# Four chunks of each input projection computed from split rows and split weights, with the VectorE taps dealt anew

## What is computed

```python
def hybrid_layer(h, p_i, prev_a, prev_c, g_mix, w_in, w_conv_a, w_s, b_s, g_ln_b, b_ln_b,
                 w_conv_c, b_conv_c, g_ln_c, b_ln_c, g_out, w_o, g_ffn, ffn,
                 g_ple, w_ple_gate, w_ple_proj):
    n = rmsnorm(h, g_mix)
    z = n @ w_in
...
    conv_a, new_a = causal_dwconv(gate_c * xa, prev_a, w_conv_a)
    y_a = gate_b * conv_a
    zb = jax.nn.gelu(z[..., o3:o4])
...
    y_b = u * chunk_mix(v, w_s, b_s)
    zc = z[..., o4:]
    glu = zc[..., :D_C] * jax.nn.sigmoid(zc[..., D_C:])
    conv_c, new_c = causal_dwconv(glu, prev_c, w_conv_c)
    y_c = jax.nn.silu(layernorm(conv_c + b_conv_c, g_ln_c, b_ln_c))
...
    h = h + y @ w_o
    h = h + ffn(rmsnorm(h, g_ffn))
```

## Time and profile before

| | us |
|---|---|
| three executions | 1082.21, 1084.42, 1085.61 |
| their median | 1084.42 |
| the profiled execution | 1082.2 |
| its span in the trace | 1080.6 |
| input projection, layer 0, in the trace | 9.4 to about 85 |
| input projection, layer 1, in the trace | 338.4 to about 416 |

### The profile page before, as it was taken

One profiled execution on the slowest core, in us unless ns is written; L12 is line 12 of the kernel. 1 busy time (PEld: TensorE's weight loads), 2 busy tenths in 40 slices (PEclk: granted clock), 3 DMA queues, 4 the chain that ended last, 5 costly groups with the idle time before them and its releaser, 6 DMA issues.

```text
span 1080.6 us, 16287 instructions
## 1 busy us (share of the span) xinstructions
PE 1063.3 (98%) x5883; PEld 921.4 (85%) x5883; DVE 886.3 (82%) x1300; ACT 682.0 (63%) x875; POOL 43.8 (4%) x58
## 2 busy tenths in 40 slices
PE   9999999999999999999999999999999999999996
PEld 8888999999999888788888888888888888878786
DVE  5898866566677888569989899898998999999775
ACT  2117544344454116458888888888888878888674
POOL 1000000000000000000010000100100001003000
PEclk9999999999999999999999999999999999999998
DMA  8442645545444433439999999999999999999921
GB/s 336 153 156 82 232 170 217 204 168 212 167 156 156 152 110 116 185 127 391 352 383 398 335 412 364 367 399 363 390 370 359 403 363 379 377 366 405 385 88 41
DMA packets 24197, 291.50 MB, mean 270 GB/s; under 512 B 3160, under 2 KB 3192, under 8 KB 7376
## 3 DMA queue, kind: packets, MB, share of 16 engines
q1 hardware_dynamic: 21040, 280.32, 67.7%
q0 software_dynamic: 3104, 10.46, 2.8%
HBM read 283.98 MB, written 6.79 MB: 269 GB/s over the span
## 4 chain that ended last, share of the span: by engine, by line
PE 92%; DVE 4%; ACT 2%; DMA 1%; issue 1%; POOL 0%; DVEq 0%; ACTq 0%; POOLq 0%
PE bank L672 16%; PE bank L676 16%; PE bank L675 15%; PE bank L721 13%; PE bank L745 8%; PE bank L748 8%; PE bank L749 8%; PE bank L761 2%; PE bank L616 1%; DMA ring<-wstream 1%; DVE cv L1498 1%; PE bank L600 1%; PE bank L581 1%; DVE wlo L1324 0%; PE bank L783 0%
## 5 line engine op out<-in xcount | busy, mean ns | idle before, releaser
L1324 DVE TENSOR_TENSOR wlo<-ring,whi 128x1024 fp32r<-128x1024 f32 x384 | 459.9, 1221 | 49.6 <-ACT whi L919 42.8
L919 ACT ACTIVATE whi<-ring 128x1024 fp32r<-128x1024 f32 x384 | 404.3, 1059 | 85.3 <-PE bank L672 72.3
L672 PE MATMUL bank<-whi,gh_hi 128*128 128x512 f32 x512 | 204.4, 399 | 0.1
L676 PE MATMUL bank<-whi,gh_lo 128*128 128x512 f32 x512 | 199.7, 390 | 0.0
L675 PE MATMUL bank<-wlo,gh_hi 128*128 128x512 f32 x512 | 199.5, 390 | 0.0
L745 PE MATMUL bank<-gh_hi,whi 128*128 128x264 f32 x480 | 138.0, 288 | 0.0
L748 PE MATMUL bank<-gh_lo,whi 128*128 128x264 f32 x480 | 136.0, 283 | 0.0
L749 PE MATMUL bank<-gh_hi,wlo 128*128 128x264 f32 x480 | 135.9, 283 | 0.0
L672 PEld LDWEIGHTS bank<-whi,gh_hi 128*128 128x128 f32 x512 | 96.2, 188 | 21.9 <-DVE wlo L1324 3.5
L676 PEld LDWEIGHTS bank<-whi,gh_lo 128*128 128x128 f32 x512 | 96.1, 188 | 20.9
L675 PEld LDWEIGHTS bank<-wlo,gh_hi 128*128 128x128 f32 x512 | 96.3, 188 | 18.4
(11 more groups left out here) (278 smaller groups left out, 1373.5 us busy)
## 6 DMA issues: line engine op xcount, KB each, us to landing
ring<-wstream SPq DMA_DIRECT2D x130, 2048.0 KB, 8.4
y_rows<-work POOLq DMA_DIRECT2D x7, 512.0 KB, 8.2
ring<-wstream SPq DMA_DIRECT2D x1, 1536.0 KB, 10.2
h<-x_in SPq DMA_DIRECT2D x2, 528.0 KB, 4.1
y_out<-work SPq DMA_DIRECT2D x2, 528.0 KB, 3.0
par<-par_in SPq DMA_DIRECT2D x2, 494.5 KB, 6.9
c_sample<-xc POOLq DMA_DIRECT2D x2, 372.0 KB, 3.6
stc<-state_in SPq DMA_DIRECT2D x2, 360.0 KB, 9.4
```

What stands on the lines that cost most here:

```text
L672: mm = pe.matmul(out[:, :], xh, whi[:, pos, cols_], start=(k == 0), stop=False)
L676: mm = pe.matmul(out[:, :], xl, whi[:, pos, cols_], start=False, stop=(k == last))
L919: nc.scalar.activation(whi[:, q % SPLITS, :], quarter_at(q), ACT.Copy).then_inc(S["hi"], 1)
L1324: v.tensor_tensor(wlo[:, q % SPLITS, :], quarter_at(q), whi[:, q % SPLITS, :].bitcast(F32), ALU.subtract).then_inc(S["lo"], 1)
```

## The change

`SPLIT_FROM = 9`: chunks `zab` 9 to 12 of both layers are computed by `project` from high and low parts of rows and weights. Their quarters drop out of `in_fp32` (`EARLY_SPLIT`), so the splitting of weights covers them. The rows' high parts, `gh_hi`, are copies of `gz` by ScalarE (`high_rows`), their low parts, `gh_lo`, subtractions by VectorE (`low_rows`); in layer 0 all eight stand behind the reciprocal root's guess, in layer 1 four ahead of it and four behind. The states are copied by ScalarE. The taps between the evacuations are 8, 8, 8, 8, then 7 and 5, then 4 each, where they were 7, 7, 7, 7, then 6 and 5 throughout. Some semaphores are merged (`ones_ready` into `consts`, `y_hi` and `y_lo` into `rows_hi` and `rows_lo`), with their counts.

```diff
+SPLIT_FROM = 9
+EARLY_SPLIT = [NEED[_b["zab"] + _c] - 1 for _b in BASE for _c in range(SPLIT_FROM, N_ZAB)]
+
+
 def in_fp32(q):
-    return any(0 <= q - a < n for a, n in zip(FP32_FROM, FP32_Q))
+    return q not in EARLY_SPLIT and any(0 <= q - a < n for a, n in zip(FP32_FROM, FP32_Q))
...
+                def projected(first, end):
+                    for c in range(first, end):
+                        if c < SPLIT_FROM:
+                            project_fp32(B["zab"] + c, 1, gz)
+                        else:
+                            project(B["zab"] + c, 1, *ghs, rows_lo if c == SPLIT_FROM else None, waited=KD * 2 * l)
+
+                projected(0, 2 * CB)
...
+                def high_rows(first, end):
+                    for k in range(first, end):
+                        act.wait_ge(S["gh_mix"], k + 1)
+                        nc.scalar.activation(gh_hi[:, k, :], gz[k], ACT.Copy).then_inc(rows_hi, 1)
+
+                if l:
+                    act.wait_ge(acc_ready, BASE[0]["ple"] + KD)
+                high_rows(0, ROWS_FIRST[l])
                 guess_of(bank[4], root[:, :], rstd[:, :], (S["ms"], 1), S["root"])
+                high_rows(ROWS_FIRST[l], KD)
+                act.wait_ge(loaded[l], 48)
+                if l:
+                    act.wait_ge(L[l - 1]["tails"], 1)
+                nc.scalar.activation(xa[:, :, :, 0:TAPS_A - 1], sta[:, :, :, :], ACT.Copy).then_inc(states_copied, 1)
+                nc.scalar.activation(xc[:, :, :, 0:TAPS_C - 1], stc[:, :, :, :], ACT.Copy).then_inc(states_copied, 1)
...
-                def states():
-
-                    dve.wait_ge(loaded[l], 48)
-                    if l:
-                        dve.wait_ge(L[l - 1]["tails"], 1)
-                    nc.vector.tensor_copy(xa[:, :, :, 0:TAPS_A - 1], sta[:, :, :, :])
-                    link(nc.vector.tensor_copy(xc[:, :, :, 0:TAPS_C - 1], stc[:, :, :, :]))
-
+                def low_rows(first, end):
+                    for k in range(first, end):
+                        dve.wait_ge(rows_hi, KD * 2 * l + k + 1)
+                        nc.vector.tensor_tensor(gh_lo[:, k, :], gz[k], gh_hi[:, k, :].bitcast(F32),
+                                                ALU.subtract).then_inc(rows_lo, 1)
+
+                low_rows(0, ROWS_FIRST[l])
                 reciprocal_root((S["root"], 1), bank[4])
+                low_rows(ROWS_FIRST[l], KD)
...
                 for c in range(2 * CB):
                     evacuate(B["zab"] + c, ycat[:, c, :])
-                    some_taps(4)
-                    low_upto(dense_quarters(B["zab"] + c))
-                    some_taps(3)
+                    some_taps(8)
...
                 for c in range(CA):
                     evacuate(at + 2 * c, pp[:, 6, :])
-                    some_taps(3)
+                    some_taps(4 if c else 7)
                     low_upto(dense_quarters(at + 2 * c))
-                    some_taps(3)
...
-                    some_taps(5)
+                    some_taps(4 if c else 5)
```

More of the change, by code:

```diff
@@ L86 @@
 EARLY_Q = (40, 45)
+ROWS_FIRST = (0, 4)
 GROUP_ORDER = (2, 0, 1)
@@ L298, in build @@
         late_step = sem("overflow_step")
+        rows_hi, rows_lo = sem("high_parts_of_rows"), sem("low_parts_of_rows")
+        states_copied = sem("states_copied")
         guessed = sem("reciprocal_root_guessed")
@@ L307, in build @@
             "y_c", "y_a", "y_b", "ys_sq", "y_ms", "y_root", "y_normed", "sq_ffn",
-            "gh_ple", "sq_ple", "sig_ple", "tails", "w_sT", "y_hi", "y_lo")} for l in range(DEPTH)]
+            "gh_ple", "sq_ple", "sig_ple", "tails", "w_sT")} for l in range(DEPTH)]
         L[0].update({n: sem(n) for n in ("gh_ffn", "silu", "hid_f32", "hid_hi", "hid", "hid2")})
@@ L424, in _ @@
             for d, t in ones.items():
-                pool.memset(t[:, :], 1.0 / d).then_inc(ones_ready, 1)
+                pool.memset(t[:, :], 1.0 / d).then_inc(consts, 1)
             pool.memset(eps[:, :], EPS).then_inc(consts, 1)
@@ L438, in _ @@
                       allow_small_or_imprecise_dtypes=True).then_inc(consts, 1)
-            pool.wait_ge(consts, 10)
+            pool.wait_ge(consts, 14)
             pool.affine_select(out=ident[:, :], in_=ident[:, :], compare_op=ALU.not_equal, fill=1.0,
@@ L724, in project_fp32, with project @@
                     mm.then_inc(acc_ready, 1)
-            def project(first_chunk, n_chunks, hi, lo, waits=None, S=dense, after=None):
+            def project(first_chunk, n_chunks, hi, lo, waits=None, S=dense, after=None, waited=0):
                 for i in range(n_chunks):
@@ L742, in project @@
                         if i == 0 and waits:
-                            pe.wait_ge(waits, k + 1)
+                            pe.wait_ge(waits, waited + k + 1)
                         wh, wl = block_of(S, q, w)
@@ L780, in _ @@
             mix = both(hid_hi, hid_lo, KD)
-            pe.wait_ge(ones_ready, len(ones))
+            pe.wait_ge(consts, len(ones))
             for _ in range(WARM_UP):
                 pe.matmul(bank[7][:, 0:P], ones[1][:, :], ones[1][:, :], start=True, stop=True)
-            pe.wait_ge(consts, 13)
+            pe.wait_ge(consts, 17)
             for l in range(DEPTH):
@@ L792, in _ @@
                 project_fp32(B["zc"] + 1, N_ZC - 1, gz)
[L793 removed]
+                def projected(first, end):
[5 more added lines that the diff above has]
+                projected(0, 2 * CB)
                 average(bank[5], D_B, [zb[:, c, :] for c in range(CB)], S["mean"], (S["gelu"], 1))
[L796 removed]
+                projected(2 * CB, 2 * CB + 2)
                 pe.wait_ge(S["squared"], 1)
                 average(bank[5], D_B, [sq[:, c, :] for c in range(CB)], S["variance"])
[L799 removed]
+                projected(2 * CB + 2, N_ZAB - 2)
                 pe.wait_ge(S["ln_b"], CB)
@@ L806, in _ @@
                 mm.then_inc(S["vt"], 1)
-                project_fp32(B["zab"] + N_ZAB - 2, 1, gz)
+                projected(N_ZAB - 2, N_ZAB - 1)
                 average_c = [cv[:, c, :] for c in range(CC)]
@@ L822, in _ @@
                 average(bank[5], D_C, [sq[:, CA + CB + c, :] for c in range(CC)], S["variance"])
-                project_fp32(B["zab"] + N_ZAB - 1, 1, gz)
+                projected(N_ZAB - 1, N_ZAB)
                 pe.wait_ge(loaded[l], 48)
@@ L845, in _ @@
                     else:
-                        project(B["wo"] + k, 1, *mix, S["y_lo"] if k == WO_FP32 else None)
+                        project(B["wo"] + k, 1, *mix, rows_lo if k == WO_FP32 else None, waited=KD * (2 * l + 1))
                     if l and k:
@@ L1033, in final_rows @@
                 nc.scalar.activation(ycat[:, k, :], h[:, k, :], ACT.Copy, scale=col(0, "g_final", k)).then_inc(y_gained, 1)
-            act.wait_ge(consts, 13)
+            act.wait_ge(consts, 17)
             nc.scalar.activation(warm[:, 0:1], eps[:, :], ACT.Abs_reciprocal_sqrt)
@@ L1107, in _ @@
                     act.wait_ge(S["y_normed"], ROW_ORDER.index(k) + 1)
-                    nc.scalar.activation(hid_hi[:, k, :], ycat[:, k, :], ACT.Copy).then_inc(S["y_hi"], 1)
+                    nc.scalar.activation(hid_hi[:, k, :], ycat[:, k, :], ACT.Copy).then_inc(rows_hi, 1)
                 for k in range(KD):
@@ L1455, in add_to_h @@
                 dve.wait_ge(acc_evac, chunk + 1)
-            dve.wait_ge(consts, 13)
+            dve.wait_ge(consts, 17)
             dve.wait_ge(par_loaded[0], 16)
@@ L1503, in _ @@
                     if c == 0:
-                        states()
+                        dve.wait_ge(states_copied, 2 * l + 2)
                     some_taps(6 if c else 0, c)
@@ L1632, in _ @@
                 for k in range(KD):
-                    dve.wait_ge(S["y_hi"], k + 1)
+                    dve.wait_ge(rows_hi, KD * (2 * l + 1) + k + 1)
                     nc.vector.tensor_tensor(hid_lo[:, k, :], ycat[:, k, :], hid_hi[:, k, :].bitcast(F32),
-                                            ALU.subtract).then_inc(S["y_lo"], 1)
+                                            ALU.subtract).then_inc(rows_lo, 1)
                 dve.wait_ge(acc_evac, B["wo"])
```

4 lines of the change are left out of this document (removed).

## The result

The changed kernel takes 1086.22 us (median, 1084.38 to 1087.62) beside 1083.79 us before (1082.21 to 1086.25, measured with it). The ratio is 1.0022 with an interval of 1.0015 to 1.0029: 1.6 to 3.1 us slower, small but real, and inside the 0.3% that was set as "no change". The forecast was +1.6 us and a median of 1086.0. Of all executions reported here one was in the chip's slower state, one of e0's twelve, with 1179.28 us at a mean granted clock of 0.85; e0's ratio leaves it out.

A forecast was written before the change was run, and what follows sets the result against it. The end of VectorE's taps, not TensorE, was taken to bound each mixer. Weight subtractions beyond VectorE's room make it 0.8 us later per layer, 2 x 0.8 = +1.6 us on 1084.42: 1086.0 us, range 1082.8 to 1089.0.

The forecast's parts named there:

- What it takes from TensorE: Four split chunks per layer: TensorE saves 1.49 us before the taps are needed, 0.43 after; 3.8 us over both layers.
- the 0.20 us for each entry: TensorE's first split matmul behind fp32 work costs 0.20 us extra; three entries per layer.
- (a): Eight VectorE subtractions per layer for the rows' low parts, costed at nothing; up to 2.8 us per layer without gaps.
- (b): Four VectorE subtractions per layer for the weights' low parts, between an evacuation and the taps' end: 1.13 us each, 4.52 us.
- Where there is room: VectorE's idle time ahead of the taps' end falls short, so the taps end 0.8 us later in each layer.
- Stretch A: VectorE, 34.78 to 57.95 in layer 0: 2.46 us idle, so five more taps, 1.98 us, fit.
- stretch B: VectorE, 57.95 to 75.39 in layer 0: 2.54 us more work against 2.12 us idle, 1.7 us of it fillable.
- Rival 1: VectorE's room suffices and the taps end within 0.2 us of before: +0.4 us or a little below; chance 0.22.
- rival 3: Eight taps per chunk don't fit under a TensorE chunk, so VectorE falls behind: +5.6 us, 1090.0; chance 0.10.
- What then: TensorE waits 1.9 us at the average on cv, losing its saving; the output projection starts 0.8 us late per layer.
- The sum: Lateness of 0.8 us in each of two layers gives +1.6 us in all.
- rival 4: TensorE's clock falls in the new wait: 2 to 4 us per layer, +5 to +9 us, about 1092; chance 0.03.

The follow-up runs named there:

- e0: The changed kernel run again with no edit, as control: 1085.41 us, ratio 1.0014 to the kernel before.
- e1: Changed kernel with the weight subtraction for chunk zab 12 moved behind the subtraction of cv's mean: 1082.75 us, ratio 0.9990 to the kernel before.
- e2: Changed kernel with the taps dealt as in the kernel before: 1091.83 us, ratio 1.0076 to the kernel before.
- e3: Changed kernel with only chunks zab 9 to 11 split, chunk 12 left in fp32: 1082.48 us, ratio 0.9989 to the kernel before.
- e6: Changed kernel with seven idle 128-column fp32 matmuls ahead of TensorE's wait for the taps: 1090.75 us, ratio 1.0059 to the kernel before.
- e8: Changed kernel with three idle 264-column fp32 matmuls ahead of TensorE's wait for the taps: 1086.75 us, ratio 1.0029 to the kernel before.
- e9: Changed kernel with no chunk split, rows' parts still made, three taps per layer moved to the last zc chunks: 1083.58 us, ratio 0.9996 to before.
- e4: Changed kernel with chunks zab 9 to 11 split and three taps per layer moved to the last zc chunks: 1080.44 us, ratio 0.9966 to before.
- e7: Changed kernel with the four weight subtractions per layer made by GpSimd instead of VectorE: 1093.9 us, ratio 1.0089 to the kernel before.

## Why the prediction was right

**What bounds.** "The end of the taps, not TensorE, sets when each layer's mixer ends." Shown by e1 (a subtraction out of the way, same work for TensorE, 2.7 us), e2 (later taps, 6.4 us more) and by the constant 20.92 to 21.00 us from the last sample-tap instruction to `wo` in every layer of before, e1, e3, e6 and e8, and in e0's layer 1: wherever this chain is the later one and the clock stayed up. One reading beside it was wrong. The prediction took TensorE for the bound "by some 0.4 us only", from the average's start at 75.89. Had it been, the first 0.4 us of the taps' delay would have cost nothing. In fact 0.81 us of delay moved `wo` by 0.81 us, since the average is not read before VectorE is through with mixer A's chunk: TensorE had some 0.56 us to spare. Once the taps end 1.3 us earlier (e9), TensorE is the bound.

**What it takes from TensorE.** 1.49 us before the taps. Measured it is 1.82 us: from the step at 63.88 in the kernel before to the average it is 12.01 us, and in the changed kernel from the same step, at 64.47, to the start of the wait, 74.66, it is 10.19. The term that was wrong is the 0.20 us for each entry from fp32 into split work. TensorE's rows behind the average on `sq`, before (it starts at 79.97) and after, show it together with the last chunk:

```profile
81.41 2.83 PE L721 MATMUL bank<-gz,ring 128*128 128x264 f32 x12
...
84.97 1.94 PE L721 MATMUL bank<-pe_in,ring 128*128 128x264 f32 x8
```

```profile
81.38 1.60 PE L767 MATMUL bank<-sq,ones 128*128 128x264 f32 x6 [1.06 <-ACT sq L1104]
82.62 0.48 PE L751 MATMUL bank<-gh_hi,whi 128*128 128x264 f32 x1
82.94 0.28 PE L754 MATMUL bank<-gh_lo,whi 128*128 128x264 f32 x1
...
85.72 1.94 PE L727 MATMUL bank<-pe_in,ring 128*128 128x264 f32 x8
```

The first split matmul does take a step of 0.32 us instead of 0.12, but it starts 0.20 us sooner behind the fp32 ones (1.24 instead of 1.44 us), so an entry costs nothing. From the average to the embedding chunk it is 5.00 us before and 4.34 after: 0.66 us saved, where 0.43 was forecast. TensorE is thus lighter by 2 x (1.82 + 0.66) = 5.0 us, not 3.8. This step carried no part of the total, since the saving went into the wait.

**What it gives to VectorE.** (a), at nothing: in layer 0 nothing of it is seen; in layer 1 the stretches stand 0.12 us later, but that goes with the splitting of weights (e9 makes the rows' parts too and does not have it), so (a) held. (b), 4 x 1.13 us: e1 moved one of the four and the taps' end moved by 1.13 us.

**Where there is room.** Stretch A took the five taps, as said. In stretch B the term was 2.54 - 1.7 = 0.8 us; measured 0.81 and 0.80. Of the wait for ScalarE's first high part, put at 0.3 us, 0.20 was there. Rival 1 (the room suffices) and rival 3 (the taps don't fit) are both out by the windows.

**What then.** TensorE's wait was put at 1.9 us, from 74.4 to 76.3. It is 2.26 us: in e0, less its start that is 0.32 us late, from 74.17 to 76.43, over the 1.5 to 2.2 us that were named as the sign. The missing 0.33 us is TensorE's larger saving.

**The sum.** 2 x 0.81 = 1.6 us. What it left out is the clock, rival 4, which was given 0.03. This is the step that was wrong, though it hardly moved the time. It rested on the row of TensorE's rest behind its last matmul, 2.3 us at clock 1.00. Of the four waits of 2.25 to 2.27 us in the changed kernel's two profiles two brought the clock down and two did not, so that one row was one draw of a thing that goes either way. Its price was wrong too: "2 to 4 us per layer" against 0.34 measured once in e0 and 0.3 in the changed kernel's layer 1. The chain behind the averages runs mostly on VectorE and ScalarE, and TensorE's slower matmuls lie in its own waits for that chain. Sum with this and the 0.12 us of layer 1: 1.6 + 0.1 + 0.3 = 2.0 us, inside the measured 1.6 to 3.1. "TensorE: Matmul & The Clock Gate" of the Trainium skill (Why this matters for your kernels) has the direction right, that a gap between bursts brings the lower level back; the traces add that it did so at 2.25 us in half of the cases, and that here it cost little.

Whether the remaining 0.4 us between 2.0 and the median's 2.4 is anything, the runs can't say. That the forecast median of 1086.0 lies so near the measured 1086.22 is in part luck: it was counted from a median of 1084.42 of three executions, and twenty gave 1083.79. The range of 1082.8 to 1089.0 does not follow from the bounds either, since 1084.4 + 5.6 is 1090.0.

## What to carry to other kernels

Before moving work off the busiest engine, find which engine is later at the point where they meet, and by how much. The meeting point is the instruction that needs both results, here VectorE's subtraction of the mean, and not the first one of the busy engine. Here TensorE was 98% busy and got 5.0 us lighter, and the kernel got slower, because VectorE, which was the later one by some 0.56 us already, paid for the saving ahead of the meeting point. Put the payer's new instructions behind that point (e1), or clear its way with idle time from farther ahead (e4); then the saving arrives. And do not split the work that stands between two gates of a chain that another engine runs (chunk 12).

## What the runs showed of the hardware

- The granted clock fell to its lower level behind two of the four waits of 2.25 to 2.27 us, in or behind all waits of 4.5 and 5.8 us (e2, e7), and behind none of 0.68 to 1.14 us at this place (e1, e3, e6, e8). In layer 0 of e2 and e7 it fell 2.0 to 2.2 us into the wait. In the router stage it fell in or behind a wait of 0.84 us in 9 of 13 executions, for about 1.6 us of the time. What differs there from the mixer's place was not tried.
- Four GpSimd subtractions of 128x1024 took 9.73 us, and VectorE's instructions with both inputs in SBUF took longer beside them: four taps 5.89 us instead of 1.66, one on 8 columns 2.31 us instead of 0.16. An evacuation from PSUM kept its 0.43 us.
- When TensorE goes from fp32 matmuls to split ones, the first split matmul takes a step of 0.32 us instead of 0.12, and it starts 0.20 us sooner behind the fp32 ones, so the passage costs nothing (changed kernel, 81.38 to 82.94).
- TensorE stood 2.90 us by "issue" 640 us behind the nearer of the two places where instructions were added (e6); why is open. Only the median of the runs and the comparison of landmarks from end to end showed it; the edited stretch looked right.
- TensorE's first projection matmul starts anywhere from 9.27 to 10.18 us, whatever the kernel. Two single profiles can differ by that and by the router's 1.6 us before any change is in them.
